# Delta scan: a level's products, masks and copies on 32 instead of 64 columns of each head

## The reference, cut to what matters

```python
kb = k * beta
a_mat = jnp.where(strict, jnp.einsum('bhnid,bhnjd->bhnij', kb, k) * decay, 0.0)
t_mat = lax.linalg.triangular_solve(eye + a_mat, eye, left_side=True, lower=True, unit_diagonal=True)
u = t_mat @ (v * beta)
w = t_mat @ (kb * jnp.exp(gc)[..., None])
def step(s, inp):                       # over the chunks
    v_new = u_i - w_i @ s
    o_i = qd_i @ s + qk_i @ v_new
    s = s * gl_i + kd_i.T @ v_new
```

## Time and profile before

| | us |
|---|---|
| median of three runs | 2608.62 (2605.36 to 2612.03) |
| the profiled execution | 2609.77 |
| its span | 2608.0 |
| TensorE busy (PE), of the span | 2504.1 (96%) |
| weight loads (PEld) | 2105.0 (81%) |
| VectorE (DVE) | 1631.6 (63%) |
| ScalarE (ACT) | 793.6 (30%) |
| GpSimd (POOL) | 1213.2 (47%) |

### The profile page before, as it was taken

The page is one execution under the profiler, slowest core; times in us unless marked ns, Lnnn a source line. Parts: engine busy times, 40 slices in busy tenths (PEclk is TensorE's granted clock), DMA queues, the critical chain, the costliest instruction groups (busy, mean ns, idle before and its releaser), DMA issues. The chain is left out here.

```text
span 2608.0 us, 45966 instructions
## 1 busy us (share of the span) xinstructions
PE 2504.1 (96%) x18822; PEld 2105.0 (81%) x18822; DVE 1631.6 (63%) x2459; ACT 793.6 (30%) x1371; POOL 1213.2 (47%) x966
## 2 busy tenths in 40 slices
PE   8999999999899999999898989999899999999998
PEld 6878888888578888878788878877898888788887
DVE  7869849751568939757665566546787236771551
ACT  4224314231534403333544254423563100210000
POOL 3555554556545455533542254322543455454553
PEclk9999999999999999999999999999999999999999
DMA  4233334322024333321101211111212322222222
GB/s 167 81 129 123 135 138 145 102 105 97 17 81 161 132 142 138 115 73 66 42 31 34 80 35 35 35 47 52 57 20 75 104 93 86 82 97 100 94 99 78
DMA packets 51176, 229.63 MB, mean 88 GB/s; under 512 B 5280, under 2 KB 12464, under 8 KB 32432
## 3 DMA queue, kind: packets, MB, share of 16 engines
q1 hardware_dynamic: 50992, 226.99, 25.3%
HBM read 224.80 MB, written 2.17 MB: 87 GB/s over the span
## 5 line engine op out<-in xcount | busy, mean ns | idle before, releaser
L246 POOL TENSOR_TENSOR ring_rounded<-ring,ring_rounded 128x512 fp32r<-128x512 f32 (+2 forms) x711 | 952.0, 1369 | 1009.8 <-DVE ring_rounded L237 720.4
L300 PE MATMUL psum<-arena_rounded,ring_rounded 128*128 128x512 f32 (+1 forms) x2820 | 1092.4, 387 | 32.8 <-DVE arena_rounded L651 10.1
L301 PE MATMUL psum<-arena_rounded,ring_rounded 128*128 128x512 f32 (+1 forms) x2820 | 1082.7, 384 | 0.0
L302 PE MATMUL psum<-arena_rounded,ring_rounded 128*128 128x512 f32 (+1 forms) x2820 | 1082.4, 384 | 0.0
L300 PEld LDWEIGHTS psum<-arena_rounded,ring_rounded 128*128 128x128 f32 x2820 | 531.0, 188 | 146.6 <-issue 22.1
L302 PEld LDWEIGHTS psum<-arena_rounded,ring_rounded 128*128 128x128 f32 x2820 | 531.0, 188 | 106.0
L301 PEld LDWEIGHTS psum<-arena_rounded,ring_rounded 128*128 128x128 f32 x2820 | 531.5, 188 | 102.8 <-issue 1.2
L237 DVE CAST ring_rounded<-ring 128x2048 fp32r<-128x2048 f32 (+5 forms) x134 | 145.6, 1087 | 477.8 <-PE psum L302 460.4
L849 ACT ACTIVATE arena<-psum,vectors 128x512 f32<-128x512 f32 x88 | 68.0, 772 | 258.1 <-DVE psum L889 258.1
L262 ACT ACTIVATE ring_rounded<-ring 128x2048 fp32r<-128x2048 f32 (+1 forms) x57 | 104.6, 1835 | 100.1 <-PE psum L302 65.5
L2268 DVE SCALAR_TENSOR_TENSOR arena<-psum,vectors,arena 128x510 f32<-128x510 f32 (+3 forms) x160 | 96.0, 638 | 12.2 <-ACT arena L2194 9.6
(11 more groups left out here) (462 smaller groups left out, 3244.6 us busy)
## 6 DMA issues: line engine op xcount, KB each, us to landing
ring<-in_w_up SPq DMA_DIRECT2D x44, 1024.0 KB, 4.9
arena<-in_w_mod SPq DMA_DIRECT2D x48, 512.0 KB, 5.5
ring<-in_w_down SPq DMA_DIRECT2D x32, 704.0 KB, 4.1
ring<-in_w_mup SPq DMA_DIRECT2D x16, 1024.0 KB, 4.9
ring<-in_w_mdown SPq DMA_DIRECT2D x16, 1024.0 KB, 4.8
ring<-in_w_gdn SPq DMA_DIRECT2D x12, 1024.0 KB, 4.8
ring<-in_w_lru_in SPq DMA_DIRECT2D x10, 1024.0 KB, 4.9
ring<-in_w_odd_in SPq DMA_DIRECT2D x10, 1024.0 KB, 4.8
```

The costliest lines, as they stand in the source:

```text
L246: last = pool.tensor_tensor(self.rounded(low), raw, self.rounded(high).bitcast(F32), ALU.subtract)
L300: pe.matmul(out, r(wh), r(xh), start=start, stop=False)
L301: pe.matmul(out, r(wh), r(xl), start=False, stop=False)
L302: return pe.matmul(out, r(wl), r(xh), start=False, stop=stop)
```

## The change

`left`, both halves of `right`, `mask`, and `x_copy` and `z_copy` from the levels on where only part of the columns can change, take 32 of each head's 64 columns: of every 2 * 2^k columns of a level (`paired`) the half that the level can change. The 64 weight columns of each product stay. As a weight, Y must be zero elsewhere, so each level gets a YC tile of its own, and POOL zeroes them once ahead of `first_level`; the tiles of levels 1 to 4 lie in part 0 of a ring slot. `negate` writes into ZC instead of YC. `m.hold` makes 24 products of the identity instead of 16.

```diff
-        b["XC"], b["YC"] = m.at(at[9], GH, HB), m.at(at[9] + GH * HB, GH, HB)
+        b["XC"] = m.at(at[9], GH, HB)
+        b["YC"] = [None] + [free[:, 2 * k + d, :, :] for k in range(LEVELS - 1)] + [m.at(at[9] + GH * HB, GH, HB)]
+    free = m.ring[:, 0, slot, :].rearrange("p (a h c) -> p a h c", h=GH, c=HB)
+    joined = lambda x: x.rearrange("p h c -> p (h c)")
+    def paired(x, k, which):
+        return x.rearrange("p (n w b) -> p n w b", w=2, b=1 << k)[:, :, which, :]
@@ left
-                        last = pe.matmul(compact(d, YB)[y, h, :], B[d]["EA"][t % 2][x, h, x], B[d]["XC"][x, h, :],
-                                         start=True, stop=True)
+                        last = pe.matmul(paired(compact(d, YB)[y, h, :], k, d), B[d]["EA"][t % 2][x, h, x],
+                                         paired(B[d]["XC"][x, h, :], k, d), start=True, stop=True)
@@ right
+                if t == 0 and k == 1:
+                    pe.wait_ge(m.sem("yzero"), m.count("yzero", 3))
...
-                        last = pe.matmul(compact(d, XB)[x, h, :], z[d][y, h, :], B[d]["YC"][y, h, :], start=False,
-                                         stop=False, skip_group_check=True)
+                        last = pe.matmul(paired(compact(d, XB)[x, h, :], k, d), z[d][y, h, :],
+                                         paired(B[d]["YC"][k][y, h, :], k, d), start=False, stop=False,
+                                         skip_group_check=True)
...
-                        last = pe.matmul(compact(d, ZB)[half[i], h, :], B[d]["YC"][y, h, :], z[d][y, h, :], start=False,
-                                         stop=False, skip_group_check=True)
+                        last = pe.matmul(paired(compact(d, ZB)[half[i], h, :], k, 1 - d), B[d]["YC"][k][y, h, :],
+                                         paired(z[d][y, h, :], k, 1 - d), start=False, stop=False,
+                                         skip_group_check=True)
@@ pe
-        m.hold(pe, 16, scan_bank(0, YB))
+        m.hold(pe, 24, scan_bank(0, YB))
@@ x_copy
-            act.activation(B[d]["XC"], compact(d, XB), ACT.Copy).then_inc(up("xcopy", d), 1)
+            x, y = joined(B[d]["XC"]), joined(compact(d, XB))
+            if k:
+                x, y = paired(x, k, d), paired(y, k, d)
+            act.activation(x, y, ACT.Copy).then_inc(up("xcopy", d), 1)
@@ z_copy
+                if k > 1:
+                    z, y = paired(z, k, 1 - d), paired(y, k, 1 - d)
@@ pool
+        def zeros():
+            pool.memset(free[:, 0:2], 0.0).then_inc(m.up("yzero"), 1)
+            pool.memset(free[:, 2:8], 0.0).then_inc(m.up("yzero"), 1)
+            for d in range(2):
+                ins = pool.memset(B[d]["YC"][LEVELS], 0.0)
+            ins.then_inc(m.up("yzero"), 1)
...
+        zeros()
         first_level(0, 0)
@@ mask
-            dve.tensor_tensor(B[d]["YC"], compact(d, YB), wide(m.lev[:, d, k, :]), ALU.mult).then_inc(up("ymask", d), 1)
+            if t == 0:
+                dve.wait_ge(m.sem("yzero"), m.count("yzero", 1 if k == 1 else 3))
+            out, y = [x.rearrange("p h (n w b) -> p h n w b", w=2, b=1 << k)[:, :, :, d, :]
+                      for x in (B[d]["YC"][k], compact(d, YB))]
+            kept = paired(m.lev[:, d, k, :], k, d).rearrange("p (a n) b -> p a n b", a=1).broadcast_to(list(out.shape))
+            dve.tensor_tensor(out, y, kept, ALU.mult).then_inc(up("ymask", d), 1)
```

More of the change, by code:

```diff
@@ L2398, in gdn_in_stage, with gdn_scan_stage @@
     run_stage(m, dict(sp=sp, pe=pe, act=act, dve=dve, pool=pool))
-def gdn_scan_stage(m, group, gc_rows):
+def gdn_scan_stage(m, group, gc_rows, slot):
     kt, qt, o = m.at(KT_AT, GH, TA), m.at(QT_AT, GH, T), m.at(O_AT, 8, T)
@@ L2413, in gdn_scan_stage @@
     klen, qhalf = m.small[:, K_LEN:K_LEN + GH * NA], m.small[:, K_HALF:K_HALF + GH * NT]
+    LEVELS = 5
+    free = m.ring[:, 0, slot, :].rearrange("p (a h c) -> p a h c", h=GH, c=HB)
     B = []
@@ L2425, in gdn_scan_stage @@
     quarter = [slice(32 * h, 32 * h + 32) for h in range(GH)]
-    LEVELS = 5
     LAST = NA - 1
@@ L2570, in far_right @@
                     near, far = half[d], half[1 - d]
-                    last = pe.matmul(compact(d, YB)[near, h, :], B[d]["YC"][far, h, :], B[d]["ZF"][far, h, far],
+                    last = pe.matmul(compact(d, YB)[near, h, :], B[d]["ZC"][far, h, :], B[d]["ZF"][far, h, far],
                                      start=True, stop=True)
@@ L2696, in z_copy @@
             if k < LEVELS:
+                z, y = joined(B[d]["ZC"]), joined(compact(d, ZB))
+                if k > 1:
+                    z, y = paired(z, k, 1 - d), paired(y, k, 1 - d)
                 if d == 0:
-                    last = act.activation(B[d]["ZC"], compact(d, ZB), ACT.Copy)
+                    last = act.activation(z, y, ACT.Copy)
                 else:
                     for i in range(2):
-                        last = act.activation(B[d]["ZC"][place(d, i)], compact(d, ZB)[half[i]], ACT.Copy)
+                        last = act.activation(z[place(d, i)], y[half[i]], ACT.Copy)
                 last.then_inc(up("zcopy", d), 1)
@@ L2831, in negate @@
             dve.wait_ge(sem("yfar", d), count("yfar", d, t + 1))
-            dve.tensor_scalar(B[d]["YC"][far], compact(d, YB)[far], -1.0, None, ALU.mult).then_inc(up("yneg", d), 1)
+            dve.tensor_scalar(B[d]["ZC"][far], compact(d, YB)[far], -1.0, None, ALU.mult).then_inc(up("yneg", d), 1)
         def residual(t, d):
@@ L4188, in second @@
         gdn_in_stage(m, S[f"gdn{g}"], S["bd"] if g == 0 else None, v, g, d["gc_rows"])
-        gdn_scan_stage(m, g, d["gc_rows"])
+        gdn_scan_stage(m, g, d["gc_rows"], unrolled(S[f"gdn{g}"])[4].slot)
     mla_in_stage(m, S["lat"], v, [(m.at(COS_AT, 2 * T + P + SEL_SIZE), d["rope"])])
```

## The result

The changed kernel takes 2615.41 us (median of 20 executions, 2608.92 to 2627.45) against 2608.77 us (20 executions, 2601.03 to 2614.65) of the kernel before. The ratio is 1.0031, 95% interval 1.0021 to 1.0040: it is slower by 6.6 us, where I had forecast 2603 us, 5.7 us faster. The profiled execution took 2613.41 us.

What follows compares the result with a forecast made beforehand. TensorE's queue was taken to bound covered levels, a chain of products, mask and copy the bare ones. Masks and copies -4.3, tails -1.6, identity products +0.2 gave -5.7: 2603 us; range 2594 to 2611.

Steps and rivals of the forecast that it cites:

- Masks and copies: VectorE and ScalarE in bare levels (nothing beside them): 128 columns in place of 256 save 2.15 us a stage, 4.3 in both.
- In covered levels it is hidden and buys nothing: Levels with other products beside: the mask ends 0.25 us before `right`, so shortening masks and copies there gains 0.
- The products: Quadrant products on TensorE: weight loads pace them, only tails at 120 array handovers shrink; 0 to 3.2 us, half taken, 1.6.
- The 24 pairs: Identity products ahead of the seeds: eight more pairs fill TensorE's pause and cost 0.1 us a stage, 0.2 in both.
- The zeros: POOL's four memsets ahead of `first_level`: about 2.4 us, done before POOL is needed, so hidden; cost 0.
- It doesn't do what it says: Rival, 8%: runs of two elements eat the masks' and copies' saving, and late zeros delay seeds up to 3.3 us a stage: 2607 to 2615.
- The clock falls more often: Rival, 22%: halved columns in bare levels bring two to five more clock falls, 2.6 to 6.5 us: 2605 to 2610.
- the signs that the prediction named: Prediction wrong if a covered level gets shorter than 3.8 us, the clock row shows new falls, or the seeds move.
- 24 pairs fill one pause: Argument against more clock falls: the added identity pairs occupy TensorE's pause of 1.72 us ahead of the seeds.
- The weight loads stay: Argument against more clock falls in bare levels: each product still loads 64 weight columns.
- The second rival: Rival, 10%: the clock falls in covered levels too; 60 us at the lower level cost 23 us: 2626 us.
- the moving columns' rival: Rival, 10%: moving columns pace quadrant products, a covered level loses 0.7 us: 2565 us, or 2583 if the mask comes next.

Runs made afterwards that it cites:

- e1: Changed kernel with all 64 moving columns back in the products; masks, copies and 24 pairs as changed: 2606.5 us, 0.9998 of the kernel before.
- e8: Kernel before with 24 identity pairs in place of 16 and nothing else: 2611.3 us, 1.0011 of the kernel before.
- e9: Changed kernel with all 64 moving columns in every product and 16 pairs, so narrow masks and copies alone: 2601.6 us, 0.9977 of the kernel before.
- e4: Changed kernel with all 64 moving columns in products of steps 0, 5 and step 1's first two levels, narrow elsewhere: 2602.8 us, 0.9985 of before.
- e5: Changed kernel with narrow products only in steps 0, 5 and step 1's first two levels, 64 columns elsewhere: 2612.6 us, 1.0023 of before.
- e3: Changed kernel with 16 identity pairs ahead of the seeds in place of 24: 2611.3 us, 1.0010 of the kernel before.
- e7: Changed kernel with 16 pairs and all 64 moving columns in products of steps 0, 5 and step 1's first two levels: 2600.4 us, 0.9968 of before.
- e10: Kernel before with its 16 identity products given 192 moving columns in place of 128: 2608.3 us, 0.9992 of the kernel before.

## Why the prediction was wrong

**The sum, at an equal clock, was near.** It said -5.7 us; the table gives 2600.7 - 2608.3 = -7.6. Its terms:

- *Masks and copies*: -4.3 forecast; -7.3 (e1 against e8) and -6.8 (e9 against before; -6.3 against the one on its own chip) measured. The two durations were right: 287 and 276 ns after, forecast 290 and 275.

```profile
L2858 DVE TENSOR_TENSOR ring<-psum,lev 128x128 f32<-128x128 f32 x96 | 23.6, 287 | 79.5 <-PE psum L2533 79.5
L2707 ACT ACTIVATE arena<-psum 128x128 f32<-128x128 f32 x120 | 26.8, 276 | 134.8 <-PE psum L2550 134.6
```

  Runs of 2 to 32 elements cost these engines nothing beyond that slope. The bare level went from 3.29 to 2.81 us, 0.48, and I had 0.26 + 0.21 = 0.47. One step was misread, "In covered levels it is hidden and buys nothing". In the earlier trace rows `right` starts 0.25 us after the masks end (1313.23 - 1312.98), and I took this for slack. In the bare level of the earlier trace rows TensorE does wait for the mask and starts 0.26 us after it (1404.90 - 1404.64): the quarter of a microsecond is the handover, and the mask was the bound, by 0.04 us. In e1 it is not, `right` starts 0.47 us behind the masks and as soon as the work beside is through (1.09 us, 1.13 before):

```profile
1306.60 0.49 DVE L2862 TENSOR_TENSOR ring<-psum,lev 128x128 f32<-128x128 f32 x2 [2.06 <-PE psum L2537]
1307.56 0.69 PE L2554 MATMUL psum<-ring,arena 64*64 64x64 f32 x32
```

  From start to start a covered level of e1 has 3.89 us (1309.74 - 1305.85). Of the undisturbed covered levels of the kernel before, about three fifths have 3.93 to 3.95 us as in the earlier trace rows, the others (beside L2581 and L2641) have 3.89 already; over 46 levels that is an estimated 1.2 us. In the waits of both stages those for the mask fell from 7.9 to 5.7 us (e9) and those of L2489 from 3.0 to 2.6, 2.6 us in all, while those for the copy of X stayed at 5.0, so the copies' share of my term does not show there. What makes up the rest of the 7 us is open.
- *The products*: -1.6 forecast, -3.9 at an equal clock (after against e1), a little beyond my full end of 3.2. The covered level of the changed kernel:

```profile
1307.47 0.67 PE L2533 MATMUL psum<-arena 64*64 64x32 f32 x32
1308.07 1.16 PE L2488 MATMUL psum<-arena 128*128 128x128 f32 x8
1309.15 0.67 PE L2550 MATMUL psum<-ring,arena 64*64 64x32 f32 x32
1309.64 0.65 PE L2559 MATMUL psum<-arena,ring 64*64 64x32 f32 x32
1310.22 1.16 PE L2488 MATMUL psum<-arena 128*128 128x128 f32 x8
1311.31 0.67 PE L2533 MATMUL psum<-arena 64*64 64x32 f32 x32
```

  Left to left 3.84 us, 0.05 less than e1; a phase of 32 is 0.67 us long in place of 0.69. The weight loads pace, as I had it (32 of them in 0.56 us in both), and the tails are what shrinks: twice 0.027 us in each level would be 0.054. I should have taken the full end, the slope of the earlier trace rows, and not the half. By halves it is less clear: e4 gains 0.8 us on e1 and e5 1.6, in sum 2.4 and not 3.9. (The Trainium skill's "TensorEngine Tiling (Array Packing)", section Instruction Overhead, gives one free column the latency of 60, by which 32 columns in place of 64 would gain nothing in the tails; the 0.05 us a level speak against it here.)
- *The 24 pairs*: +0.2 forecast, +3.6 measured (e8). I had costed the pairs in the place where they stand, and there they do cost nothing. What failed is that the sum ended at the seeds: 16 more records in TensorE's queue were felt behind them.
- *The zeros*: 0 forecast, 0 found. POOL's rows of the changed kernel:

```profile
1263.13 0.53 POOL L2767 MEMSET ring<- 128x512 f32 x1 [1.08 <-POOLq L605]
1263.60 1.38 POOL L2768 MEMSET ring<- 128x1536 f32 x1
1264.91 0.57 POOL L2770 MEMSET arena<- 128x256 f32 x2
...
1267.84 0.73 POOL L2793 TENSOR_TENSOR arena<-arena,eye 128x256 f32<-128x256 f32 x1 [1.31 <-DVE arena L2841]
1268.71 0.69 PE L2509 MATMUL psum<-ident,arena 64*64 64x64 f32 x32
```

  The memsets end after 2.35 us (I had taken 2.4), POOL still waits for VectorE, and the seeds start 5.54 us after the stage, 5.53 before. This part of "It doesn't do what it says" fell, and so did the part on short runs.

**The clock was not.** The step that failed is the clock's term: the sum has none, and the rival "The clock falls more often" held it at 22% and at "Two to five more falls: 2.6 to 6.5 us". Measured are some 41 us at the lower level of the two stages in place of 3.4, and about 16 us. The mechanism stands in that rival, with the right levels and the right reason (half of the array's work gone from the bare levels), and its price for each us was right: 1.3 / 3.39 = 0.38 by the earlier trace rows (three phases of 1.13 us), 0.38 by the slope of the runs. What was mis-sized is how long the falls last. I priced a fall as one event of 1.3 us, the length of the one fall in the kernel before; here the lower level held for 10 to 14 us three times. By the mean clock (0.9921 to 0.9840) it is 2 x 0.0081 x 2613 = 42 us more at the lower level and 1960 x 0.0081 = 15.9 us, against a gain of 7.6 at an equal clock. That these two make up the 8.2 us between the means is how the split is built and shows nothing. The lengths of the stages show it: from e1 to the changed kernel they grow by 13.0 us, though its covered levels at the upper clock are 0.05 us shorter, an estimated 3 us in 60 levels, so the falls cost some 16 us; 0.38 x 41 is 15.6. Of the signs that the prediction named, this one showed (new falls in the clock row), and neither of the others (a covered level below 3.8 us, seeds that move). My two arguments against it fell as well. "24 pairs fill one pause": e3 has 0.986 with 16 of them. "The weight loads stay": they do, in e1 as in the changed kernel, and the clock is 0.991 in the one and 0.984 in the other.

The second rival, falls that reach the covered levels, was half right: the low stretches do run over covered levels, and that is what makes them dear. But in the changed kernel they start in or right behind bare ones, and narrow products in covered levels alone (e4) leave the mean clock where it was. It was priced at 60 us and 23 us; 42 and 16 were found. What of the moving columns' rival remains is the 0.05 us a level.

## What to carry to other kernels

Taking columns away from TensorE's products can cost more than it saves where these products stand alone in a chain of waits: before you narrow them, look in the trace for a stretch like it that already has fewer columns and see what clock it was granted, and price a fall by all the work that follows it, not by one phase. Narrow what VectorE and ScalarE do in such a chain, and leave its products as they are (e9: 2601.6 us, 0.9977 [0.9965, 0.9989]); narrow products where other full products surround them did no harm (e7: 2600.4 us, 0.9968 [0.9956, 0.9981]), and what they add is not clear of the noise. A short gap between one engine's end and the next one's start is no slack until you have seen how long the same handover takes where the engine does wait. Price instructions added to a full queue beyond the place where they stand: if time on the engine is all that is wanted, fewer and wider instructions gave it here for nothing (e10).

## What the runs showed of the hardware

- Half the moving columns, with instructions, weight loads and waits unchanged, moved the mean granted clock from 0.991 to 0.984 (e1 to after); the profiled executions have some 41 us at 1.2 GHz in the two stages after, and 3.4 before. Weight loads at an unchanged rate did not hold the clock up.
- At the lower level eight 128x128 products took 2.07 us in place of 1.16, a phase of 32 quadrant products 1.08 in place of 0.67; for each us at that level 0.38 us were lost over whole executions, and 0.44 in a covered level (6.88 us in place of 3.84).
- Products in four quadrants of 64x64 with 32 and with 64 moving columns follow each other at the same pace (a phase of 32 records 0.67 and 0.69 us).
- Sixteen more records on TensorE ahead of each of the two stages (24 pairs in place of 16) cost 2.5 to 3.6 us in all, and the same array time in fewer records nothing; from 16 to 8 pairs nothing was gained.
- TensorE's products start 0.25 us after the end of the VectorE instruction that they wait for (0.26 in the earlier trace rows).
- POOL's memsets of 512, 1536 and 256 columns took 0.53, 1.38 and 0.29 us each; VectorE and ScalarE take 287 and 276 ns for 128 fp32 columns in runs of 2 to 32, where the slope of long rows gives 290 and 275.
